# Setup folded into the first layer, and its conditioning groups dealt out anew

## The chip, the cores and the metric

One core of a Trainium2 chip runs the whole program. The metric is the device time of one execution in microseconds; the median of three is what is compared. TensorE (PE) multiplies, VectorE (DVE), ScalarE (ACT) and GpSimd (POOL) do the rest, SyncE (SP) issues most loads.

## What is computed

Two blocks of a network over 512 tokens of width 1024, all in float32. The first block projects x into 28 tiles of 128 features and mixes them in five ways (a short gated convolution, a spatial gating unit, a multi-scale pooling, a 31-tap convolution, an attention over 256 memory tokens), gates the result and projects it out. The second block conditions its norms on a vector c, and this is what the change moves about:

```python
cond = jax.nn.silu(c)
for layer in range(DEPTH_2):
    mod = (cond @ ada_w[layer] + ada_b[layer])[:, None, :]
    shift1, scale1, gate1, shift2, scale2, gate2 = jnp.split(mod, 6, axis=-1)
    hn = rmsnorm(x, norm1_w[layer]) * (1 + scale1) + shift1
```

`cond @ ada_w` for both layers is, for the two layers together, a vector times a 1024 x 12288 matrix that is read once; the kernel computes it in twelve groups of 1024 outputs, off TensorE, beside other stages.

## The kernel before

The program is a row of stages, each a block of five instruction streams (one for each engine) with a boundary behind it: no engine enters a stage before all have left the last. `stage_setup` (L420) loads memory, key/value weights and x from SP, seventeen small tables from ACT, clears tables in device memory from POOL, and takes the Silu of c once all small tables are there. `stage_first` (L511) makes keys and values (4 blocks of weights), then 28 projections of one weight block each (`project`, 16 matmuls, float32 in two passes); between them PE does the small products of the five mixers in an order written out by hand, and ACT (`take`) and DVE follow in orders of their own. `stage_out` (L904) is the output projection in eight blocks, then a layer norm and a first RMS norm. `stage_ffn` (L1356) is the feed-forward with its own seven conditioning groups.

Weights stream through a ring of eight slots, filled by SP in order of use: `load_first` (L183) gives the first eight orders, each behind the use that frees its slot. PSUM's banks 0 and 1 take the projections in turn, banks 2 to 7 the small products.

A conditioning group is eight chunks of weights (128 x 1024, 512 KB), each multiplied by one element of `cond` per partition and added to a sum. On DVE (`weigh`, L484) a chunk is one instruction (L490; the first of a group L488), on POOL two (L580, L581; the first L578). Chunks lie in four buffers; two of them share their place with the memory tile, so that their loads wait for the last key/value block. A finished sum goes over PE: `spread_sums(c)` issues eight narrow products (sixteen matmuls, L506), and `finish_conditioning` (L493) adds the bias on DVE. Before the change, in the first layer DVE makes group 0 before anything else and POOL groups 1 to 4, with two buffers for the sums, so that POOL's group c (from 2 on) waits until group c-2 has been spread.

DVE's order in the first layer: group 0; the input product (L829) and the taps of the long convolution (L800, two instructions a tap) with softmax(0) and softmax(1) between them (L808 to L814); `norm_v.centre` (L320); the pooling (L819 to L859); `norm_v.invert` (L324) and the scaling of v (L862 to L864), which PE's `turn_values` (L643) waits for; then the rest. PE's `turn_probs(j)` (L624) waits for softmax(j).

Of the kernel before, what the change touches and what calls it, by code (L numbers as in the profile page):

```python
# [11 lines left out]
P = 128  # L12
S = 512
ST = S // P
# [93 lines left out]
class Chip:  # L108


    def __init__(self, nc, ctx):
# [42 lines left out]
        self.vlink, self.alink, self.glink, self.plink = (Link(self.sem(n)) for n in  # L154
                                                          ("dve_step", "act_step", "pool_step", "pe_step"))
# [264 lines left out]
def stage_setup(m, a):  # L420
    nc = m.nc
    m.s_small, m.s_x, m.s_mem, m.s_gel, m.s_const = (m.sem(n) for n in ("small_loaded", "x_loaded", "mem_loaded",
                                                                        "table_loaded", "consts_set"))
    m.s_zero = m.sem("table_cleared")
    m.memT = m.W[:, 14:18, :].rearrange("p a (b c) -> p (a b) c", c=MEM)
    with nc.Block() as block:  # L426
        @block.sync
        def _(sp):
            sp.dma_start(m.memT, a["memT"]).then_inc(m.s_mem, 16)
            load_first(m, sp, m.plans["kv"])  # L430
            sp.dma_start(m.X[:], a["xT"]).then_inc(m.s_x, 16)

        @block.scalar
        def _(act):
            for out, src in ((m.par[:], a["par"]), (m.cst[:], a["cst"]), (m.lvl[:], a["lvl"]), (m.sel[0:HEADS], a["sel"]),
                             (m.sel[32:32 + HEADS], a["sel"]),
                             (m.sgw[:], a["sgw"]), (m.plw[0:64, 0, 0:64], a["plw"][0]),
                             (m.plw[64:128, 0, 64:128], a["plw"][1]), (m.plw[0:64, 1, 0:64], a["plw"][2]),
                             (m.plw[64:128, 1, 64:128], a["plw"][3]), (m.pw[:], a["pw"]), (m.gw[:], a["gw"]),
                             (m.rw[:], a["rw"])):  # L440
                act.dma_start(out, src).then_inc(m.s_small, 16)

            for h in range(4):
                act.dma_start(m.sgb[64 * (h % 2):64 * (h % 2) + 64, h // 2, :],
                              a["sgb"][h].partition_broadcast(64)).then_inc(m.s_small, 16)
            m.n_small = 17 * 16
            act.wait_ge(m.s_small, m.n_small)
            nc.scalar.activation(m.cond[:], m.p("c"), ACT.Silu).then_inc(m.alink.sem, 1)
            m.alink.n += 1
            act.wait_ge(m.alink.sem, m.alink.n)  # L450

        @block.vector
        def _(dve):
            step = m.vlink.on(dve)
            for t, v in ((m.ones128, 1 / P), (m.ones256, 1 / DG), (m.ones1024, 1 / D), (m.ones, 1.0)):
                step(nc.vector.memset(t[:], v))

        @block.gpsimd
        def _(pool):
            step = m.glink.on(pool)  # L460
            for lo, j in ((0, 64), (64, 0)):
                step(nc.gpsimd.memset(m.plw[lo:lo + 64, :, j:j + 64], 0.0))

            for r in range(EXPERTS):
                step(nc.gpsimd.memset(m.rank_caps[:, r:r + 1], float(CAPS[r])))
                step(nc.gpsimd.memset(m.rank_first[:, r:r + 1], float(FIRST[r])))
            step(nc.gpsimd.memset(m.zero[:], 0))
            pool.dma_start(m.d_tokens.rearrange("(e r) o -> e (r o)", e=EXPERTS), m.zero[:]).then_inc(m.s_zero, 16)
            blank = m.W[0:ROWS - sum(CAPS), 0:2, :]
            step(nc.gpsimd.memset(blank, 0.0))  # L470
            for rest in [m.d_first[FIRST[-1]:, :]] + [m.d_result[p * ROWS + sum(CAPS):(p + 1) * ROWS, :]
                                                      for p in range(PASSES - 1)]:
                pool.dma_start(rest, blank.rearrange("p a c -> p (a c)")).then_inc(m.s_zero, 16)
            pool.wait_ge(m.s_zero, 16 * (1 + PASSES))


# [4 lines left out]
GROUPS, EARLY_GROUPS = 12 * D // COND, 5  # L481
# [29 lines left out]
def stage_first(m):  # L511
# [20 lines left out]
    mx, nmx, rs, ri = ((lambda h, i=i: stat(h, i)) for i in range(4))  # L532
    chunk_in = m.chunk_in = [m.sem(f"cond_loaded{i}") for i in range(CHUNKS)]
    m.chunk_used, m.acc_ready, m.acc_done = (m.sem("cond_" + n) for n in ("used", "summed", "out"))
    chunk_used, acc_ready, acc_done = m.chunk_used, m.acc_ready, m.acc_done
# [6 lines left out]
    with nc.Block() as block:  # L542
        @block.sync
        def _(sp):
            load_first(m, sp, inn)
            load_rest(m, sp, inn)
            load_first(m, sp, out)

        @block.gpsimd
        def _(pool):  # L550
            step = m.glink.on(pool)
            for h in range(4):
                last = nc.gpsimd.tensor_tensor(m.sgw[:, h, :], m.sgw[:, h, :], m.c("tri"), ALU.mult)
                give(pool, last, masked, h + 1)
            step(nc.gpsimd.memset(m.gates_w[:], 0.0))
            for j in range(2):
                step(nc.gpsimd.tensor_copy(m.gates_w[:, :, 32 * j:32 * j + HEADS], m.gw[:, :, rows(j, HEADS)]))
# [3 lines left out]

            load(0)
            load(1)
            pool.wait_ge(m.blocks_done, kv.done + kv.n)
            load(2)
            load(3)
            for n in range(CHUNKS, KD + CHUNKS):
                pool.wait_ge(chunk_used, n - CHUNKS + 1)
                load(n)
            for c in range(1, EARLY_GROUPS):  # L570
                if c >= 2:
                    pool.wait_ge(acc_done, c - 1)
                for k in range(KD):
# [8 lines left out]
                    if n + CHUNKS < EARLY_GROUPS * KD:  # L582
                        load(n + CHUNKS)
# [3 lines left out]
        def _(pe):  # L587
# [31 lines left out]
            def turn_probs(j):  # L619
                for i in range(2):  # L620
# [78 lines left out]
            project(CA)  # L699
            norm_c.var(m, pe)  # L700
            project(CA + 1)
# [3 lines left out]
            project(GATES[1])  # L705
            pointwise()
            for name in GATES[2:6]:
                project(name)
            spread_sums(3)
            for name in GATES[6:]:  # L710
                project(name)
            spread_sums(4)

        @block.scalar
        def _(act):
            step = m.alink.on(act)
            for b in range(4):
# [36 lines left out]
            for name in (DA, DA + 1, DGT, DGT + 1, Q, Q + 1):  # L754
                take(name)
            exps(0)
            take(V)
            take(V + 1)
            take_probs(0)
            take(U)  # L760
            take_attended(0)
            exps(1)
            take(U + 1)
            take(XC)
            take_probs(1)
# [1721 lines left out]
```

## Time and profile before

| | us |
|---|---|
| median of 3 runs | 2237.7 |
| lowest, highest | 2235.6, 2239.43 |
| the profiled execution, its own time | 2241.91 |
| its span | 2239.6 |
| PE busy | 2143.4 |
| DVE busy | 717.2 |
| ACT busy | 518.1 |
| POOL busy | 438.8 |

The times of the views are microseconds from the start of the span. A line of a timeline gives start, length, engine, line of the kernel, operation, output and inputs, shape, count, and in brackets how long the engine had been idle and what released it. Neighbouring instructions of one form are merged; the length then covers them all. The granted clock of TensorE is a share of 2.4 GHz.

### The profile page before, as it was taken

What the parts mean: (1) busy time and instruction counts of PE and PEld (TensorE: products, weight loads), DVE (VectorE), ACT (ScalarE), POOL (GpSimd) and SP (SyncE); (2) the same over time, 40 slices, a digit from 0 to 9 for tenths busy, and PEclk for the clock granted to TensorE, in tenths of its full rate; (3) what the DMA queues carried; (4) which work ended last, traced back from release to release, by engine and by line L of the source; (5) the groups of instructions that cost most, each with busy time, mean ns of one, the idle gap of its engine ahead of it and who ended that gap; (6) DMA issues with size and microseconds to landing.
All of it is one profiled execution on the core that took longest, in us unless ns stands there. A gap on an engine that the chain in (4) does not pass through costs nothing. (4 is left out here: it accounts for less than half of the span.)

```text
span 2239.6 us, 24940 instructions
## 1 busy us (share of the span) xinstructions
PE 2143.4 (96%) x9870; PEld 1441.3 (64%) x9870; DVE 717.2 (32%) x966; ACT 518.1 (23%) x885; POOL 438.8 (20%) x367
## 2 busy tenths in 40 slices
PE   5898999999999999999999999999999999999997
PEld 3343445556554444446444667675599999999996
DVE  1786212345562232320002466676210000000013
ACT  0231001434332000000002666753112111111101
POOL 2829921100001111100000444453120000000011
PEclk9999998899999999997999999999999999999998
DMA  7524331111103555522211211110196577778882
GB/s 282 192 73 132 115 111 46 38 48 57 57 29 113 163 194 191 193 87 105 75 61 56 67 48 57 53 42 19 66 319 196 191 248 236 232 267 296 316 337 97
DMA packets 81230, 308.18 MB, mean 138 GB/s; under 512 B 9832, under 2 KB 10352, under 8 KB 80864
## 3 DMA queue, kind: packets, MB, share of 16 engines
q1 hardware_dynamic: 60768, 238.05, 31.5%
q0 software_dynamic: 16800, 59.87, 8.0%
q10 hardware_dynamic: 3552, 8.74, 1.1%
q8 instruction: 76, 1.25, 0.2%
q14 instruction: 34, 0.28, 0.0%
HBM read 297.30 MB, written 9.33 MB: 137 GB/s over the span
## 5 line engine op out<-in xcount | busy, mean ns | idle before, releaser
L244 PE MATMUL banks<-sb_x_norm,sb_ring 128*128 128x512 f32 x1344 | 588.8, 597 | 3.9 <-ACT sb_x_norm L401 3.9
L2092 PE MATMUL banks<-sb_act,sb_ring 128*128 128x192 f32 (+3 forms) x3696 | 502.9, 299 | 3.0 <-issue 2.9
L2092 PEld LDWEIGHTS banks<-sb_act,sb_ring 128*128 128x128 f32 x3696 | 500.0, 191 | 4.5 <-issue 4.2
L244 PEld LDWEIGHTS banks<-sb_x_norm,sb_ring 128*128 128x128 f32 x1344 | 254.1, 191 | 312.2 <-issue 309.2
L244 PE MATMUL banks<-sb_x_res,sb_ring 128*128 128x512 f32 x448 | 197.0, 598 | 0.0
L2370 DVE TENSOR_TENSOR sb_act<-sb_work,banks 128x128 f32<-128x128 f32 (+3 forms) x88 | 27.7, 315 | 518.0 <-PE banks L2092 496.4
L244 PE MATMUL banks<-sb_act,sb_ring 128*128 128x512 f32 x352 | 153.4, 599 | 3.1 <-PEq L1367 3.1
L244 PEld LDWEIGHTS banks<-sb_x_res,sb_ring 128*128 128x128 f32 x448 | 85.5, 193 | 104.8 <-issue 104.8
L356 POOL TENSOR_TENSOR sb_work<-sb_work 128x512 f32<-128x512 f32 x18 | 22.8, 1265 | 555.7 <-ACT sb_work L348 555.7
L244 PEld LDWEIGHTS banks<-sb_act,sb_ring 128*128 128x128 f32 x352 | 67.6, 192 | 88.1 <-issue 88.1
L255 PEld LDWEIGHTS banks<-sb_ring,sb_x_norm 128*128 128x128 f32 x1024 | 116.0, 192 | 2.5 <-issue 2.4
L255 PE MATMUL banks<-sb_ring,sb_x_norm 128*128 128x128 f32 x1024 | 117.0, 275 | 0.0
L1016 PE MATMUL banks<-sb_act,sb_ring 128*128 128x512 f32 x256 | 112.4, 594 | 0.4 <-DVE sb_act L1752 0.4
L244 PE MATMUL banks<-sb_work,sb_ring 128*128 128x512 f32 (+1 forms) x192 | 81.1, 588 | 27.2 <-PEq L426 25.3
L1964 POOL DMA_INDIRECT sb_work<-first_expert_rows,sb_table x8 | 7.5, 938 | 463.8 <-DMA first_expert_rows<-sb_x_norm 461.7
L2199 ACT ACTIVATE sb_work<-banks 128x128 f32<-128x128 f32 (+3 forms) x88 | 26.3, 298 | 308.5 <-PE banks L2092 306.0
L1709 POOL TENSOR_TENSOR sb_act<-sb_act 128x512 f32<-128x512 f32 x56 | 80.6, 1438 | 65.6 <-PE banks L1554 28.4
L1695 POOL TENSOR_TENSOR sb_act<-sb_act 128x512 f32<-128x512 f32 x56 | 60.6, 1083 | 145.6 <-DVE sb_act L1759 93.8
L1016 PEld LDWEIGHTS banks<-sb_act,sb_ring 128*128 128x128 f32 x256 | 47.8, 190 | 61.2 <-issue 59.4
L1413 DVE TENSOR_TENSOR sb_act<-sb_work,banks 128x512 f32<-128x512 f32 x22 | 15.1, 686 | 213.9 <-PE banks L244 213.9
L244 PEld LDWEIGHTS banks<-sb_work,sb_ring 128*128 128x128 f32 x192 | 39.0, 204 | 68.2 <-issue 66.8
L1554 PEld LDWEIGHTS banks<-sb_act 128*128 128x128 f32 x512 | 62.7, 192 | 24.8 <-issue 17.1
(368 smaller groups left out, 2158.8 us busy)
## 6 DMA issues: line engine op xcount, KB each, us to landing
sb_ring<-in_w_moe_up SPq DMA_DIRECT2D x176, 512.0 KB
sb_ring<-in_w_moe_down SPq DMA_DIRECT2D x64, 704.0 KB
sb_work<-in_cond_w POOLq DMA_DIRECT2D x48, 512.0 KB, 4.7
sb_ring<-in_w_ffn_up SPq DMA_DIRECT2D x44, 512.0 KB
sb_ring<-in_w_h_in SPq DMA_DIRECT2D x32, 512.0 KB
sb_ring<-in_w_in SPq DMA_DIRECT2D x28, 512.0 KB
sb_act<-in_cond_w POOLq DMA_DIRECT2D x28, 512.0 KB, 4.9
sb_ring<-in_w_m_in SPq DMA_DIRECT2D x24, 512.0 KB
```

What stands on the lines that cost most here:

```text
L244: last = m.nc.tensor.matmul(bank[:, 0:act.shape[2]], w[:, rows(k, P)], act[:, k, :], start=(k == 0), stop=(k == kt - 1))
L255: last = m.nc.tensor.matmul(bank[:, rows(t, P)], act[:, k, rows(t, P)], w[:, rows(k, P)], start=(k == 0), stop=(k == kt - 1))
L356: m.nc.gpsimd.tensor_tensor(self.acc, self.acc, self.sq[:, k % 2, :], ALU.add).then_inc(m.rms_sum, 1)
L1016: last = m.nc.tensor.matmul(m.ps[:, b % BANKS, :], m.ring[:, s, rows(k, P)], act_in[:, k, :], start=(k == 0), stop=(k == kt - 1))
L1413: nc.vector.tensor_tensor(out, W[:, s % 2:s % 2 + 1, :], ps[:, (2 * s + 1) % BANKS:(2 * s + 1) % BANKS + 1, :], ALU.mult).then_inc(m.evac, 2)
L1554: last = nc.tensor.matmul(ps[:, 2 + n % 2, rows(t, P)], lhs[:, rows(t, P)], rhs[:, rows(t, P)], start=True, stop=True)
L1695: give(pool, nc.gpsimd.tensor_tensor(H[:, n % 2, :].rearrange("p (n c) -> p n c", c=2 ** j), b, b[:, :, half - 1:half].broadcast_to([P, S ...
L1709: give(pool, nc.gpsimd.tensor_tensor(H[:, 4 + n % 2, :], k_of(h), H[:, n % 2, :], ALU.mult), k_ready, n)
L1964: nc.gpsimd.indirect_dma_start(got[2 * t + j], None, table, bass.IndirectOffsetOnAxis(ap=m.table[:, c:c + 1], axis=0)).then_inc(gathered[t ...
L2092: last = nc.tensor.matmul(ps[:, b % BANKS, 0:cap], w, act, start=(k == 0), stop=(k == kt - 1))
L2199: nc.scalar.activation(silu_t[j % 2][:, 0:cap], ps[:, 2 * j % BANKS, 0:cap], ACT.Silu).then_inc(silu, 1)
L2370: nc.vector.tensor_tensor(hid[:, j, 0:cap], silu_t[j % 2][:, 0:cap], ps[:, (2 * j + 1) % BANKS, 0:cap], ALU.mult).then_inc(m.evac, 2)
```

## The change

`stage_setup` is gone. Its loads stand at the head of `stage_first`: SP's before the projection weights; ACT's in two parts, `par` and `cst` at once, the other tables behind the memory tile, and `lvl`, `sel` and `rw` not before `stage_out`. POOL's clearing of tables goes to `stage_out`. Engines wait for the tables by semaphores of their own (`s_par`, `s_small`, `s_x`, `s_cond`). In the first layer POOL makes groups 0 to 2 and DVE none; DVE makes groups 3 and 4 in `stage_out`, three chunks behind each block, with loads issued by ACT; PE spreads them behind block 6. The feed-forward keeps seven. The orders of PE, ACT and DVE in the first layer shift: each small product comes about one projection later relative to the blocks, softmax(0) comes after `taps(1, 5)`, softmax(1) after `taps(5, 16)`, `norm_v.centre` after `taps(16, 26)`, and v is finished before most of the pooling. In the experts' stage four semaphores are merged into others. The core of it:

```diff
 stage_first, sync
+            sp.dma_start(m.memT, a["memT"]).then_inc(m.s_mem, 16)
+            load_first(m, sp, kv)
+            sp.dma_start(m.X[:], a["xT"]).then_inc(m.s_x, 16)
             load_first(m, sp, inn)
 stage_first, gpsimd
+            pool.wait_ge(m.s_x, 16)
+            load(0)
+            load(1)
+            pool.wait_ge(m.s_small, N_SMALL)
...
-            for n in range(CHUNKS, KD + CHUNKS):
-                pool.wait_ge(chunk_used, n - CHUNKS + 1)
-                load(n)
-            for c in range(1, EARLY_GROUPS):
+            pool.wait_ge(m.s_cond, 1)
+            for c in range(FIRST_GROUPS):
 stage_first, tensor
             project(V + 1)
+            project(U)
             turn_probs(0)
-            project(U)
+            project(U + 1)
             attend(0)
             scores(1)
-            project(U + 1)
             project(XC)
+            project(XC + 1)
             turn_probs(1)
-            project(XC + 1)
+            project(XA)
             attend(1)
             norm_v.mean(m, pe)
             spread_sums(0)
             spread_sums(1)
-            project(XA)
+            project(XA + 1)
             norm_v.var(m, pe)
-            project(XA + 1)
             project(BA)
+            project(BA + 1)
             turn_values()
-            project(BA + 1)
+            project(CA)
             gating()
...
-            spread_sums(3)
...
-            spread_sums(4)
 stage_first, scalar
+            act.dma_start(m.par[:], a["par"]).then_inc(m.s_par, 16)
+            act.dma_start(m.cst[:], a["cst"]).then_inc(m.s_small, 16)
+            act.wait_ge(m.s_par, 16)
+            nc.scalar.activation(m.cond[:], m.p("c"), ACT.Silu).then_inc(m.s_cond, 1)
+            act.wait_ge(m.s_mem, 16)
...
 stage_first, vector
-            for k in range(KD):
-                dve.wait_ge(chunk_in[k % CHUNKS], 16 * (k // CHUNKS + 1))
-                weigh(m, step, chunk[k % CHUNKS], sums[0], k)
-                dve.sem_inc(chunk_used, 1)
-            dve.sem_inc(acc_ready, 1)
-            taps(1, 9)
+            taps(1, 5)
             softmax(0)
-            taps(9, 16)
+            taps(5, 16)
             softmax(1)
-            taps(16, TAPS_D - 1)
+            taps(16, 26)
+            norm_v.centre(m, dve)
+            taps(26, TAPS_D - 1)
 stage_out, tensor
+            def spread_sums(b):
+                if b == KD - 2:
+                    for c in range(FIRST_GROUPS, EARLY_GROUPS):
+                        pe.wait_ge(m.acc_ready, c + 1)
+                        spread_group(m, sums[c - FIRST_GROUPS], 7, c).then_inc(m.acc_done, 1)
 stage_out, vector
             for b in range(plan.n):
...
+                for n in range(per * b, min(per * (b + 1), loads)):
+                    conditioning(n)
+                if b == KD - 2:
+                    dve.wait_ge(m.acc_done, EARLY_GROUPS)
+                    finish_conditioning(m, step, FIRST_GROUPS, EARLY_GROUPS,
+                                        ps[:, 7, 8 * FIRST_GROUPS:8 * EARLY_GROUPS], ((0, 1, "norm2"),))
 stage_out, scalar
+            for n in range(loads):
+                if n >= CHUNKS:
+                    act.wait_ge(m.chunk_used, n - CHUNKS + 1)
+                act.dma_start(chunk[n % CHUNKS], m.cond_w[begun + n]).then_inc(chunk_in[n % CHUNKS], 16)
             nc.scalar.preload_act_table(ACT.Sqrt)
```

## Rows read from the trace of the kernel before

**Rows 1.** The page: busy time and share of the engines.
```profile
PE 2143.4 (96%) x9870; PEld 1441.3 (64%) x9870; DVE 717.2 (32%) x966; ACT 518.1 (23%) x885; POOL 438.8 (20%) x367
```
**Rows 2.** Waits of TensorE, 0 to 400 us: total, times, longest.
```profile
PE banks L643 <- DVE sb_act L864: 10.4, 1, 10.4
PE banks L624 <- DVE sb_act L814: 8.8, 2, 7.4
```
**Rows 3.** Timeline of TensorE, 20 to 300 us.
```profile
25.30 9.39 PE L244 MATMUL banks<-sb_work,sb_ring 128*128 128x256 f32 x32 [25.30 <-PEq L426]
41.67 18.62 PE L244 MATMUL banks<-sb_x_res,sb_ring 128*128 128x512 f32 x43
...
83.73 2.00 PE L614 MATMUL banks<-sb_act 64*128 64x256 f32 x16 [0.69 <-ACT sb_act L730]
...
107.10 1.97 PE L624 MATMUL banks<-sb_cst,sb_act 128*128 128x128 f32 x8 [7.44 <-DVE sb_act L814]
...
120.65 1.94 PE L635 MATMUL banks<-sb_act 128*64 128x512 f32 x8
...
187.11 1.97 PE L643 MATMUL banks<-sb_cst,sb_act 128*128 128x128 f32 x8 [10.37 <-DVE sb_act L864]
...
293.33 1.95 PE L506 MATMUL banks<-sb_ones,sb_x_norm 128*128 128x1 f32 x16
297.19 71.75 PE L244 MATMUL banks<-sb_work,sb_ring 128*128 128x512 f32 x160 [1.91 <-PEq L542]
```
**Rows 4.** Timeline of ScalarE: the Silu in setup.
```profile
24.46 0.21 ACT L448 ACTIVATE sb_cond<-sb_par 128x8 f32<-128x8 f32 x1 [11.69 <-DMA sb_sgb<-in_sgb]
```
**Rows 5.** DMA, 0 to 25 us: traffic; size and us from issue to landing.
```profile
DMA packets 2768, 7.97 MB, mean 319 GB/s; under 512 B 808, under 2 KB 1328, under 8 KB 2512
...
sb_x_res<-in_xT SPq DMA_DIRECT2D x1, 2048.0 KB, 18.8
sb_work<-in_memT SPq DMA_DIRECT2D x1, 1024.0 KB, 5.5
```
**Rows 6.** Timeline of VectorE, 69 to 156 us.
```profile
69.97 2.15 DVE L829 TENSOR_TENSOR sb_act<-sb_act 128x1024 f32<-128x1024 f32 x1 [9.01 <-ACT sb_act L730]
...
74.01 25.47 DVE L800 SCALAR_TENSOR_TENSOR sb_work<-sb_act,sb_par,sb_work 128x511 f32<-128x511 f32 x16
...
110.42 10.81 DVE L800 SCALAR_TENSOR_TENSOR sb_work<-sb_act,sb_par,sb_work 128x503 f32<-128x503 f32 x14
124.63 1.23 DVE L808 TENSOR_REDUCE sb_small<-banks 128x4 f32<-128x1024 f32 x1 [3.40 <-PE banks L614]
...
133.75 22.10 DVE L800 SCALAR_TENSOR_TENSOR sb_work<-sb_act,sb_par,sb_work 128x496 f32<-128x496 f32 x28
```
**Rows 7.** Timeline of GpSimd: the first instruction of groups 1, 2 and 3.
```profile
61.99 2.85 POOL L578 TENSOR_SCALAR sb_x_norm<-sb_x_norm,sb_cond 128x1024 f32<-128x1024 f32 x1
...
152.63 2.92 POOL L578 TENSOR_SCALAR sb_x_norm<-sb_x_norm,sb_cond 128x1024 f32<-128x1024 f32 x1 [42.44 <-PE banks L506]
...
200.14 2.86 POOL L578 TENSOR_SCALAR sb_x_norm<-sb_x_norm,sb_cond 128x1024 f32<-128x1024 f32 x1
```
**Rows 8.** Timeline of VectorE: inside the pooling, inverse of v, last gate.
```profile
165.13 0.69 DVE L852 COPY sb_work<-sb_act 64x512 f32<-64x512 f32 x1
...
178.13 3.35 DVE L324 RECIPROCAL sb_act<-sb_act 128x512 f32<-128x512 f32 x1
...
293.99 0.69 DVE L898 TENSOR_TENSOR sb_work<-sb_work,sb_act 128x512 f32<-128x512 f32 x1 [5.91 <-ACT sb_act L730]
```
**Rows 9.** Window behind a stall: length, busy PE, PEld, DVE, ACT, POOL, clock, DMA.
```profile
107.10:112.20 5.10, 3.72 (x16) 3.32 (x17) 4.07 (x5) 4.04 (x8) 2.80 (x2) 0.50 0.20 48
```
**Rows 10.** Timeline of TensorE: two spreads.
```profile
150.68 3.63 PE L506 MATMUL banks<-sb_ones,sb_x_norm 128*128 128x1 f32 x32
```
**Rows 11.** Timeline of VectorE: a weighing; the page: loads of chunks.
```profile
50.62 1.28 DVE L490 SCALAR_TENSOR_TENSOR sb_x_norm<-sb_work,sb_cond,sb_x_norm 128x1024 f32<-128x1024 f32 x1 [1.33 <-DMA sb_work<-in_cond_w]
...
sb_work<-in_cond_w POOLq DMA_DIRECT2D x48, 512.0 KB, 4.7
```

More of the change, by code:

```diff
@@ L417 @@
 YA, YB, YC, YD, YE = 0, 2, 4, 6, 8
[L420 to L474, printed above, removed]
@@ L551, in _, with load @@
             step = m.glink.on(pool)
+            for lo, j in ((0, 64), (64, 0)):
+                step(nc.gpsimd.memset(m.plw[lo:lo + 64, :, j:j + 64], 0.0))
+            for r in range(EXPERTS):
+                step(nc.gpsimd.memset(m.rank_caps[:, r:r + 1], float(CAPS[r])))
+                step(nc.gpsimd.memset(m.rank_first[:, r:r + 1], float(FIRST[r])))
+            step(nc.gpsimd.memset(m.gates_w[:], 0.0))
+            def load(n):
+                pool.dma_start(chunk[n % CHUNKS], m.cond_w[n]).then_inc(chunk_in[n % CHUNKS], 16)
+            pool.wait_ge(m.s_x, 16)
+            load(0)
+            load(1)
+            pool.wait_ge(m.s_small, N_SMALL)
             for h in range(4):
@@ L619, in turn_probs @@
             def turn_probs(j):
+                if j == 0:
+                    pe.wait_ge(m.s_small, N_SMALL)
                 for i in range(2):
@@ L705, in _ @@
             project(GATES[1])
+            project(GATES[2])
             pointwise()
-            for name in GATES[2:6]:
+            for name in GATES[3:6]:
                 project(name)
-            spread_sums(3)
             for name in GATES[6:]:
                 project(name)
-            spread_sums(4)
         @block.scalar
@@ L787, in _ @@
             give(act, last, conv_act, 1)
-            for name in GATES[1:]:
+            for name in GATES[2:]:
                 take(name)
@@ L909, in stage_out @@
     total, sq = m.W[:, 12, :], m.W[:, 13:15, :]
+    wide = lambda t: t.rearrange("p a c -> p (a c)")
+    chunk = [wide(m.A[:, 2 * i:2 * i + 2, :]) for i in range(CHUNKS)]
+    sums = [wide(m.A[:, 2 * i:2 * i + 2, :]) for i in range(CHUNKS, CHUNKS + EARLY_GROUPS - FIRST_GROUPS)]
+    chunk_in = [m.sem(f"ln_cond_loaded{i}") for i in range(CHUNKS)]
+    begun, loads, per = FIRST_GROUPS * KD, (EARLY_GROUPS - FIRST_GROUPS) * KD, 3
     std, inv = m.small[:, 48:48 + ST], m.small[:, 52:52 + ST]
@@ L920, in _ @@
         def _(pool):
+            step = m.glink.on(pool)
+            step(nc.gpsimd.memset(m.zero[:], 0))
+            pool.dma_start(m.d_tokens.rearrange("(e r) o -> e (r o)", e=EXPERTS), m.zero[:]).then_inc(m.s_zero, 16)
+            blank = m.W[0:ROWS - sum(CAPS), 15:17, :]
+            step(nc.gpsimd.memset(blank, 0.0))
+            for rest in [m.d_first[FIRST[-1]:, :]] + [m.d_result[p * ROWS + sum(CAPS):(p + 1) * ROWS, :]
+                                                      for p in range(PASSES - 1)]:
+                pool.dma_start(rest, blank.rearrange("p a c -> p (a c)")).then_inc(m.s_zero, 16)
             for k in range(1, KD - 1):
@@ L958, in _, with conditioning @@
         def _(dve):
+            step = m.vlink.on(dve)
+            def conditioning(n):
+                c, k = divmod(n, KD)
+                dve.wait_ge(chunk_in[n % CHUNKS], 16 * (n // CHUNKS + 1))
+                weigh(m, step, chunk[n % CHUNKS], sums[c], k)
+                dve.sem_inc(m.chunk_used, 1)
+                if k == KD - 1:
+                    dve.sem_inc(m.acc_ready, 1)
             for b in range(plan.n):
@@ L1885, in stage_moe @@
         "last_slots", "last_slots_turned", "last_slots_out", "early_turned", "last_mixed", "added", "early_mixed"))
-    gathered = [m.sem(f"e_early{t}") for t in range(ST)]
     got_sem = [m.sem(f"e_gathered{i}") for i in range(BUFS)]
@@ L2329, in mix @@
             def mix(t, turn):
-                dve.wait_ge(gathered[t], 32 * turn)
+                for i in (2 * t, 2 * t + 1):
+                    dve.wait_ge(got_sem[i], 16 * ((1 if turn == 1 else PASSES) * got_used[i] - (i == 0) + turn))
                 a1, a2 = got[2 * t], got[2 * t + 1]
```

93 lines of the change are left out of this document (54 added, 39 removed).

## The prediction

> **What bounds the kernel now.** The page first: TensorE (PE) is busy 96% of a 2239.6 us span [rows 1]. Time can come only from PE's gaps or its work, and the change leaves PE's work as it is: the same blocks, the same twelve groups of conditioning. So the question is which gaps lie in the three stages touched, the first 400 us. PE's waits there name two behind VectorE (DVE): 10.4 us at L643 (`turn_values`) and 8.8 us at L624 (`turn_probs(0)`) [rows 2]; its timeline adds a third, 25.30 us before the first matmul. It projects from 41.67, and begins the output stage at 297.19 [rows 3]. The first gap is the block boundary behind setup: the Silu of ScalarE (ACT) waits until 24.46 for the last small table [rows 4], and PE starts 0.84 us later. What PE itself needs, the memory tile and weight block 0, was there long before: the memory tile landed 5.5 us after its order, at about 6.4 [rows 5]. The other two gaps are a late DVE: from 69.97 it hardly rests, and its taps take 25.47/16 = 1.59 us each while GpSimd (POOL) computes, but 22.10/28 = 0.79 us while it is idle [rows 6, 7].
>
> I count from T0, the first projection (41.67 in the old trace). A block of 16 matmuls is 6.87 us: six take 83.73 - 0.69 - 41.67 = 41.4 with the last one's tail [rows 3].
>
> **The head.** PE now needs the memory tile (6.4) and block 0 of the key weights, 0.52 MB behind it in the same queue. The first 25 us moved 0.319 MB/us on average [rows 5]: 1.6 us alone, 3.3 us if ACT's tables take half, so PE starts between 8.0 and 9.7; I take 8.5. Its four key/value blocks take 41.67 - 25.30 = 16.4 us [rows 3], so T0 = 24.9, 16.8 earlier. What this hides must be there in time. The input X: ahead of it or beside it go 1.05 MB (memory), 2.1 (weights), 2.1 (X itself) and 1.5 (ACT's tables), 6.75 MB, at 0.319 MB/us 21 us, against 24.9. Without that cover T0 moves one for one. ACT's orders of the tables: all seventeen ended by 24.46 - 11.69 = 12.8 us, a table load included [rows 4]; now eleven of them start behind the memory tile, which bounds their end by 6.4 + 12.8 = 19 and, by their share, puts it at 14; ACT's first copy of keys is due at 14.5, and PE's fourth block would be the first to feel it. Setup's memsets on DVE and POOL lie beside loads: nothing.
>
> The Trainium skill's "DMA: Bandwidth & Descriptors", under Queues, rings and completion order, says that each DMA engine serves the queues it has work for in turn, a packet at a time. By it ACT's tables could take up to half of block 0's turns, and PE would start at 9.7, not 8.5: the sum would be 1.2 us smaller.
>
> **Three groups on POOL, none on DVE in the first stage.** DVE loses eight weighings, but it sat idle for 9.01 us before L829, waiting for a projection [rows 6], so that buys nothing. POOL began its first group 20.3 us behind the old T0 (61.99); now it begins when the key/value blocks are done and two chunks are ordered, 1 us behind T0. A group takes 200.14 - 152.63 = 47.5 us [rows 7]. It computes from T0+1 to T0+96 without a rest, where before it did from T0+20 to T0+68 and again from T0+111. So DVE's taps meet it longer.
>
> **DVE's chain in the new order, from T0.** The projection it starts from is ready at 69.97 - 41.67 = 28.3. Products and bias, 74.01 - 69.97 = 4.0 -> 32.3. `taps(1,5)`, 8 instructions at 1.59 = 12.7 -> 45.0. The scores are there at 83.73 + 2.00 - 41.67 = 44.1, so softmax(0) runs at once: 110.42 - 99.48 = 10.9 -> 55.9. PE wants its probabilities after one more block than before, at 64.9: that gap is closed. `taps(5,16)`, 22 at 1.59 = 35.0 -> 90.9, all beside POOL. Softmax(1): 133.75 - 124.63 = 9.1 beside an idle POOL, 10.9 beside a busy one [rows 6]; half of it is beside POOL, and the higher is nearer as ACT loads a table in it: 10.9 -> 101.8. `taps(16,26)`, 20 at 0.79 = 15.8 -> 117.6: POOL is idle, its third group waiting for `spread_sums(0)` at 117.5 (below). Centring, one pass over 128x1024 out of PSUM like L808 (1.23) -> 118.8. `taps(26,30)`, 8 at 1.59 -> 131.5. The last two taps and two doublings: 165.13 - 155.85 = 9.3 held these and a centring, so 8.1 -> 139.6. Inverse and scaling of v, 187.11 - 178.13 = 9.0 -> 148.6 [rows 3, 8]. The rest of the pooling, 178.13 - 165.13 = 13.0, now stands behind v.
>
> **PE against it.** PE comes to 73.5 through `turn_probs(0)` (1.75) and one more block, attend and scores(1), 3.8 -> 77.3, two blocks -> 91.0. There `turn_probs(1)` needs probabilities whose softmax only begins at 90.9: the old gap again, at the other half. The old one took 120.65 - (107.10 - 7.44) = 21.0 us for 8.6 us of work (transposes 1.75, a block 6.87) [rows 3]; part of its price is the clock, 0.50 of 2.4 GHz in the 5.1 us behind that idleness [rows 9]. Taken over: loss 12.4, PE at 112.0. Attend 1.9, a mean about 1.8, two spreads 3.6 [rows 3, 10] -> 119.3 (the first spread ends at 117.5), three blocks and a variance 22.3 -> 141.6. `turn_values` waits for DVE until 148.6: 7.0 us. So the stage's end hangs on DVE: from `turn_values` to the last block the old PE took 293.33 - 187.11 = 106.2 [rows 3], now one block (6.87) and one spread (1.8) less: 97.6 -> 246.2. POOL's third group ends at T0 + 117.5 + 47.5 = 165, before PE asks for it at 179.
>
> **Into the output stage.** Behind the last block ACT and DVE still take 294.68 - 293.33 = 1.35 us [rows 8], then three small steps instead of five and the boundary, 1.91 less 0.4 [rows 3]: 2.9. Start: 24.9 + 246.2 + 2.9 = 274.0 against 297.19, 23.2 earlier. There two spreads stand between blocks 6 and 7: 3.63 us of PE [rows 10]. DVE gets three weighings of 1.28 a block besides its 0.7, 4.5 us in 71.75/8 = 9.0 of PE's block: hidden; without that cover each of six blocks would wait. Chunks land in 4.7 us [rows 11] and are ordered a block ahead (four buffers, three used a block) by ACT, whose own work there is the norm behind block 7; the last of its sixteen orders waits for the twelfth chunk, in block 3. POOL clears tables before its first addition, under blocks 0 and 1. In the experts' stage only the semaphore waited for changes; the feed-forward keeps seven groups. Nothing for either.
>
> **Sum.** -23.2 + 3.6 = -19.6 us. The profiled execution took 2241.91 us for a span of 2239.6, the median of the runs is 2237.7, and a difference of spans holds for either: 2237.7 - 19.6 = 2218.1.
>
> **Bounds.** PE's start 8.0 to 9.7, or 12 if its first instructions come slowly; softmax(1) 9.1 to 10.9; 38 contended taps, four of which fit one turn of POOL's two instructions, so that a phase is worth a tap at each change of neighbour, in all some 4 us either way; the clock's share of the loss 0 to 4.8 (12.4 - 7.44 and rounding). Together 2209 to 2227.
>
> **Rivals.**
> (a) *VectorE is held up less.* If contention cost nothing, both PE gaps close and PE's own work decides: 12.4 + 7.0 = 19.4 more, 2198.7. For it: the free tap of 0.79. Against it: the same two forms of instruction met from 74 to 99.5 and a tap took 1.59.
> (b) *The loads don't come in order.* If the first weight block lands only with the whole stream, at 21 us, PE starts 4.3 us earlier, not 16.8: 2230.6. Against it: the memory tile landed in 5.5 us where X, behind it, took 18.8 [rows 5].
> (c) *DVE's chain is 10 to 20 us longer*, since more of it stands beside POOL than before and contended operations scatter: 2228 to 2238. No row asks for it.
> (d) *Slower.* DVE loses each GpSimd instruction entire. It would then get two operations into a turn of POOL's two instructions (47.5/8 = 5.9 us, 6.4 beside taps) where the trace shows four: 3.2 us a tap, 61 us more for 38 taps, 2279. It decides from about 20 us of added delay, 13 such taps. Against it: 1.59 a tap is in the rows with the same neighbour [rows 6, 7].
> The Trainium skill's "SBUF — State Buffer", Who interferes with whom, states the rule of (d): the two engines share a pair of ports under a lock held for a whole instruction, and the loser fully blocks. The trace agrees that they meet, but not that a whole instruction is lost each time.
> (e) *The head's change does nothing*: no wait is left in front of PE but the tile and the block, so no chance of its own.
>
> **Chances.** Forecast 0.72, (a) 0.10, (b) 0.06, (c) 0.09, (d) 0.03. To hold eight in ten the range takes the forecast's bounds and the near parts of (a) and (c): 2207 to 2229. A measurement of this kernel tells 0.2% (4.5 us) from no change. Faster: the forecast, (a), (b) and half of (c), 0.92; same 0.05; slower 0.03.
>
> **What would show it.** First matmul at 8.5, T0 at 25; no gap at `turn_probs(0)`, one of about 8 us at `turn_probs(1)` with a granted clock near 0.5 behind it, 7 us at `turn_values`; taps at 1.59 until POOL's second group ends; the output stage from 274, two spreads between its blocks 6 and 7 without a wait; all later stages shifted as they are. It is wrong if the first projection waits for X, PE for POOL's third group, or a block of the output stage for DVE.

## The result and the profile after

The changed kernel takes 2219.8 us (median of 4, 2217.5 to 2224.0) where the kernel before, beside it, takes 2236.65 (2235.3 to 2239.4): the medians stand 16.9 us apart. This document goes by the ratio of the executions, 0.9919, with a 95% interval of 0.9901 to 0.9937, which is 18.1 us of 2237 (14.1 to 22.1); it is not the quotient of the medians, here or below. The forecast was 2218.1 with 2207 to 2229. The profiled execution took 2218.68 us for a span of 2217.0.

The page's busy time of each engine, to be held against rows 1: TensorE (PE) does what it did and 2.8 us more, VectorE (DVE) 17.6 us more, GpSimd (POOL) 42.7 us less.

```profile
PE 2146.2 (97%) x9870; PEld 1441.9 (65%) x9870; DVE 734.8 (33%) x975; ACT 517.2 (23%) x884; POOL 396.1 (18%) x336
```

The waits of PE from 0 to 400 us: total, times, longest. Rows 2 had 10.4 and 8.8 us behind DVE and, in front of all, the 25.30 us of rows 3. Now it is 8.9 for the first weights, 8.1 at `turn_probs` (L580) and 2.6 at `turn_values` (L599).

```profile
PE banks L243 <- DMA sb_ring<-in_w_kv: 8.9, 1, 8.9
PE banks L580 <- DVE sb_act L783: 8.1, 2, 7.7
PE banks L243 <- PEq L488: 3.2, 1, 3.2
PE banks L599 <- DVE sb_act L824: 2.6, 1, 2.6
```

PE's timeline shows where these stand (start, length, and in brackets the idle time and its releaser):

```profile
8.93 10.14 PE L243 MATMUL banks<-sb_work,sb_ring 128*128 128x256 f32 x32 [8.93 <-DMA sb_ring<-in_w_kv]
...
26.04 41.37 PE L243 MATMUL banks<-sb_x_res,sb_ring 128*128 128x512 f32 x96
...
124.94 1.97 PE L580 MATMUL banks<-sb_cst,sb_act 128*128 128x128 f32 x8 [7.71 <-DVE sb_act L783]
...
144.21 8.81 PE L243 MATMUL banks<-sb_x_res,sb_ring 128*128 128x512 f32 x16
...
171.11 1.17 PE L599 MATMUL banks<-sb_cst,sb_act 128*128 128x128 f32 x8 [2.65 <-DVE sb_act L824]
...
271.95 63.23 PE L243 MATMUL banks<-sb_work,sb_ring 128*128 128x512 f32 x140 [3.18 <-PEq L488]
335.02 3.63 PE L449 MATMUL banks<-sb_ones,sb_act 128*128 128x1 f32 x32
338.51 10.53 PE L243 MATMUL banks<-sb_work,sb_ring 128*128 128x512 f32 x20
```

The first projection (T0) starts at 26.04 instead of 41.67, the output stage at 271.95 instead of 297.19 [rows 3]: 25.2 us earlier. Of that 7.0 go again before `stage_m`, the mixer behind the output stage: its first full block starts at 398.13, against 416.37 before (18.2 earlier). The feed-forward's first block is as much earlier (703.56 against 721.74), and so are the late blocks of the experts' stage (up to 2123.36 against 2141.41). The spans stand 22.6 us apart; the 4.5 us more arise behind that point, in a tail of 98.2 us before and 93.6 now, with 2.0 us less waiting of PE (9.3 and 7.3 us from 2000 us on). In the ten further traces below, all with the changed experts' stage, this tail takes 92.2 to 96.9 us, so most of the 4.5 is scatter; whether the four merged semaphores add to it, no run separates.

DVE's timeline:

```profile
58.66 12.74 DVE L769 SCALAR_TENSOR_TENSOR sb_work<-sb_act,sb_par,sb_work 128x511 f32<-128x511 f32 x8
71.44 1.22 DVE L777 TENSOR_REDUCE sb_small<-banks 128x4 f32<-128x1024 f32 x1
72.69 2.34 DVE L778 TENSOR_SCALAR sb_small<-sb_small 128x4 f32<-128x4 f32 x1
...
82.74 35.32 DVE L769 SCALAR_TENSOR_TENSOR sb_work<-sb_act,sb_par,sb_work 128x507 f32<-128x507 f32 x22
...
127.31 15.28 DVE L769 SCALAR_TENSOR_TENSOR sb_work<-sb_act,sb_par,sb_work 128x496 f32<-128x496 f32 x20
142.63 1.22 DVE L319 TENSOR_TENSOR sb_act<-sb_act,banks 128x1024 f32<-128x1024 f32 x1
143.77 10.60 DVE L769 SCALAR_TENSOR_TENSOR sb_work<-sb_act,sb_par,sb_work 128x486 f32<-128x486 f32 x8
```

Here and below a tap is one instruction; the kernel's `taps(a, b)` issues two for each step, so `taps(5, 16)` is 22. A tap costs 12.74/8 = 1.59 and 35.32/22 = 1.61 us beside POOL, 15.28/20 = 0.76 beside an idle one. POOL's group 2 starts at T0 + 116.6, released by a spread:

```profile
142.66 2.84 POOL L532 TENSOR_SCALAR sb_x_norm<-sb_x_norm,sb_cond 128x1024 f32<-128x1024 f32 x1 [18.03 <-PE banks L449]
```

In the output stage three weighings a block take 4.92 us, dearer than 3 x 1.28, and DVE still idles over 3 us before the next block:

```profile
309.47 0.69 DVE L960 SCALAR_TENSOR_TENSOR sb_x_res<-sb_x_res,banks 128x512 f32<-128x512 f32 x1 [3.50 <-PE banks L243]
310.07 4.92 DVE L433 SCALAR_TENSOR_TENSOR sb_act<-sb_act,sb_cond 128x1024 f32<-128x1024 f32 x3
```

### The profile page after: what moved, and what is told of

It reads as the page before. It is cut to its first block and busy times, and to the rows that moved or that the text cites. A ratio compares the mean times of both kernels' runs of the same rounds, so it can differ in the third digit from the quotient of the medians.

```text
span 2217.0 us, 24937 instructions
## 1 busy us (share of the span) xinstructions
PE 2146.2 (97%) x9870; PEld 1441.9 (65%) x9870; DVE 734.8 (33%) x975; ACT 517.2 (23%) x884; POOL 396.1 (18%) x336
## 5 line engine op out<-in xcount | busy, mean ns | idle before, releaser
L1567 PEld LDWEIGHTS banks<-sb_act 128*128 128x128 f32 x512 | 62.7, 192 | 25.1 <-issue 17.4
```

Source lines behind the costliest of these rows:

```text
L1567: last = nc.tensor.matmul(ps[:, 2 + n % 2, rows(t, P)], lhs[:, rows(t, P)], rhs[:, rows(t, P)], start=True, stop=True)
```

## The experiments

The theory: three things make up the gain and the loss. The head gives 16 us; DVE is held up by POOL and so keeps PE waiting twice; the spreads moved to the output stage cost there what they cost. Rivals: head and order don't add up, since one hides the other; the two stalls are a matter of DVE's order, not of POOL. Ratios are to the kernel before, run beside each, with 95% intervals. Edits are shown against the changed kernel, and only their core.

**e1_head_alone**: the changed kernel's head, with the groups and the orders of before.

```diff
-GROUPS, FIRST_GROUPS, EARLY_GROUPS = 12 * D // COND, 3, 5
+GROUPS, FIRST_GROUPS, EARLY_GROUPS = 12 * D // COND, 5, 5
...
-            taps(1, 5)
+            taps(1, 9)
```

> The kernel before with only the loads merged into the first stage (POOL's clearing in the output stage too); DVE makes group 0, POOL groups 1 to 4, all orders of the first stage as before. My theory: the head and the rest add up, and relative to the first projection nothing changes. First matmul at 8.9, first projection at 26.0 as in the changed kernel (15.6 earlier than 41.67), gaps of about 8.8 and 10.4 us at turn_probs(0) and turn_values remain, ratio to before 2222/2237.7 = 0.993 (0.9925 to 0.9935). Rival: the head is worth more or less with the old dealing, because POOL and DVE now work beside a DMA queue that is still full at the head; then the gaps differ from 8.8 and 10.4 by more than 2 us.

Measured: 2229.19 us, 0.9947 (0.9927 to 0.9967), 11.9 us (7.4 to 16.3), less than expected. T0 comes at 25.80, 15.9 us earlier, but the output stage only 13.6 and `stage_m`'s first block 14.8:

```profile
95.83 3.65 PE L583 MATMUL banks<-sb_cst,sb_act 128*128 128x128 f32 x16 [12.05 <-DVE sb_act L786]
...
172.89 1.97 PE L602 MATMUL banks<-sb_cst,sb_act 128*128 128x128 f32 x8 [8.68 <-DVE sb_act L841]
...
283.58 70.60 PE L243 MATMUL banks<-sb_work,sb_ring 128*128 128x512 f32 x160 [1.81 <-PEq L488]
```

The wait at `turn_probs(0)` is 12.05 us where rows 3 have 7.44 with a second one of 1.4 behind it: 3.2 us more, which is what the rival named (over 2 us). POOL works beside that softmax in both kernels, but DVE meets other instructions of it. Counted from T0, PE gets its probabilities 4.6 us later: 1.2 us because the first product takes 3.32 us for 2.15, 1.4 us in a wait for ScalarE (1.78 for 0.43), and 2.0 us because the first scaling of the probabilities takes 3.21 us for 1.22. From T0 to the output stage it is 257.8 us against 255.5. So in this trace the head's gain isn't passed on whole while the old order stands.

**e2_head_undone**: the rest of the change, with its loads in a block of their own ahead of the first layer (the tables `lvl`, `sel` and `rw` and the clearing stay in the output stage).

```diff
+    with nc.Block() as block:
+        @block.sync
+        def _(sp):
+            load_first(m, sp, inn)
...
+            act.wait_ge(m.s_cond, 1)
+            act.wait_ge(m.s_x, 16)
```

> The changed kernel with the head's loads in a block of their own that ends when they have landed; new groups and orders kept. My theory: first matmul at about 20 to 25, and every later time relative to the first projection as in the changed kernel; the rest of the change is worth 18.1 - 15.6 = 2.5 us, ratio to before 0.998 to 0.9995. Rival: regrouping and orders are what pays, then the ratio is under 0.996.

Measured: 2230.11 us, 0.997 (0.9949 to 0.9991), 6.7 us (2.0 to 11.4), between the forecast and its rival. Its ten executions reach from 2227.7 to 2241.9 us, four of them above 2235. PE starts at 21.41: the block for setup alone is 3.9 us shorter than the old one.

```profile
21.41 8.95 PE L243 MATMUL banks<-sb_work,sb_ring 128*128 128x256 f32 x32 [21.41 <-PEq L488]
...
136.18 1.97 PE L610 MATMUL banks<-sb_cst,sb_act 128*128 128x128 f32 x8 [7.65 <-DVE sb_act L801]
```

11.9 and 6.7 us make 18.6, the whole change 18.1: within the intervals, which are wide, the parts add up, and nothing here speaks for parts that hide one another. Some 3.9 us of e2's gain is that shorter block, not order or groups, which by the ratios leaves these about 3. The trace says more: from T0 to `stage_m`'s first block e2 takes 364.6 us where the kernel before takes 374.7, so 10.1 less, and the changed kernel's two traces 372.1 and 365.7 (the second is e8's, below). What order and groups bring by themselves is therefore open between some 3 and 10 us.

**e3_light_gpsimd**: in chunks 1 to 7 of its groups 0 and 1 POOL computes 128 of 1024 columns (the rest of the conditioning of these chunks is left out), with the same loads and waits.

```diff
                     else:
+                        if c < 2:
+                            src, total = src[:, 0:P], total[:, 0:P]
```

> The changed kernel, but in groups 0 and 1 POOL multiplies and adds only the first 128 of 1024 columns of chunks 1 to 7 (that part of the conditioning is left out); loads, waits and the third group stay. My theory: POOL's work beside DVE is what makes DVE late. Taps near 0.79 us until the third group, the softmax of heads 2 and 3 done before PE asks, both PE gaps (7.7 + 0.4 and 2.65 us) closed and the slower clock behind them gone: the first stage ends 13 to 16 us earlier, ratio to the changed kernel's 0.9919 lower by 0.006 to 0.007, so about 0.985 to before. Rival: DVE is late by its order, not by POOL; then at least 5 us of the gap at turn_probs(1) stays.

Measured: 2207.35 us, 0.9857 (0.9829 to 0.9886), as forecast. POOL is through with the two groups at 66.2 us, the same 22 taps take half, and PE finds its probabilities and v ready:

```profile
69.94 0.17 DVE L780 TENSOR_SCALAR sb_small<-sb_small 128x4 f32<-128x4 f32 x1
...
77.81 17.07 DVE L771 SCALAR_TENSOR_TENSOR sb_work<-sb_act,sb_par,sb_work 128x507 f32<-128x507 f32 x22
101.89 1.22 DVE L779 TENSOR_REDUCE sb_small<-banks 128x4 f32<-128x1024 f32 x1 [7.02 <-PE banks L570]
```
```profile
115.54 1.91 PE L582 MATMUL banks<-sb_cst,sb_act 128*128 128x128 f32 x16
...
155.74 1.09 PE L601 MATMUL banks<-sb_cst,sb_act 128*128 128x128 f32 x8
...
254.89 63.37 PE L243 MATMUL banks<-sb_work,sb_ring 128*128 128x512 f32 x140 [3.19 <-PEq L488]
```

From T0 (24.52) to the output stage it is 230.4 us against 245.9. With the order unchanged, both stalls go when POOL's work goes: they are POOL's doing, and this is what is left to win in the stage, 15.5 us.

**e4_second_softmax_early**: softmax(1) ten taps earlier, to close the wait at `turn_probs(1)`.

```diff
-            taps(5, 16)
+            taps(5, 11)
             softmax(1)
-            taps(16, 26)
+            taps(11, 26)
```

> The changed kernel with taps(5,11) before softmax(1) and taps(11,26) behind it, nothing else. My theory: the end of the first stage hangs on the whole of DVE's chain to v, not on each gap by itself. The gap at turn_probs(1) closes (PE 11 us earlier there), POOL's third group starts 11 us earlier and so lies beside more taps, v is ready 0 to 8 us later than 171.1, and PE waits for it at turn_values for 14 to 22 us instead of 2.65: ratio to before 0.992 to 0.996, no better than the changed kernel. Rival: each gap has its own price, and closing this one gives 8 to 11 us: ratio 0.987 to 0.988.

Measured: 2229.88 us, 0.9951 (0.9935 to 0.9968). The wait is gone, and two others, of 19.6 us together, stand behind it (PE's waits, 0 to 400 us):

```profile
PE banks L292 <- ACT sb_act L304: 11.1, 1, 11.1
PE banks L243 <- DMA sb_ring<-in_w_kv: 9.1, 1, 9.1
PE banks L599 <- DVE sb_act L824: 8.6, 1, 8.6
```

The earlier attend lets the spread through earlier, so POOL's third group starts at 131 and holds up DVE's thirty taps (36.35 us), and the centring behind them is late for `norm_v.var` (L292). I had put the whole delay at `turn_values`; the place was wrong, the size (19.6 against 14 to 22) and the ratio were not. The rival, that each gap has a price of its own (0.987 to 0.988), falls.

**e5_two_groups** and **e6_two_groups_reordered**: only groups 0 and 1 in the first layer, group 2 on DVE in the output stage; e6 also places softmax(1), the centring and the finishing of v where PE wants them.

```diff
-GROUPS, FIRST_GROUPS, EARLY_GROUPS = 12 * D // COND, 3, 5
+GROUPS, FIRST_GROUPS, EARLY_GROUPS = 12 * D // COND, 2, 5
...
-            spread_sums(2)
...
-    begun, loads, per = FIRST_GROUPS * KD, (EARLY_GROUPS - FIRST_GROUPS) * KD, 3
+    begun, loads, per = FIRST_GROUPS * KD, (EARLY_GROUPS - FIRST_GROUPS) * KD, 4
```
```diff
# e6 beside that; v's inverse, product and scaling move up
-            taps(5, 16)
+            taps(5, 11)
             softmax(1)
-            taps(16, 26)
+            taps(11, 18)
             norm_v.centre(m, dve)
-            taps(26, TAPS_D - 1)
+            taps(18, 25)
+            norm_v.invert(m, dve)
...
+            taps(25, TAPS_D - 1)
```

> The changed kernel with two groups on POOL in the first stage and three on DVE in the output stage (four weighings a block instead of three). My theory: the gap at turn_values was POOL's third group beside the chain to v, that at turn_probs(1) the first two. So the first stays (7 to 8 us at turn_probs(1)), the gap of 2.65 at turn_values closes, v is ready 8 to 12 us earlier than 171.1, the output stage's DVE still keeps up (0.7 + 4 x 1.28 = 5.8 of 8.6 us a block): 2.5 to 4.5 us better than the changed kernel run beside it, 0.998 to 0.999 of it. Rival: DVE can't hide a third group in the output stage, a block waits there, and it is slower than the changed kernel by 3 us or more.

> As the run with two groups, and DVE's order changed: taps(5,11), softmax(1), taps(11,18), centring of v, taps(18,25), inverse and scaling of v, the other taps, pooling. My theory (the chain as a whole is what counts, and it is now short enough): both gaps and the wait for the centred v that showed when softmax(1) alone was moved are closed, PE has no wait above 1 us between its first projection and the output stage, which starts 11 to 15 us earlier than in the changed kernel: ratio to before 0.985 to 0.988. Rival: as with softmax(1) moved alone, the time comes back as another wait behind DVE, and the gain over the changed kernel is under 5 us.

Measured: e5 2218.83 us, 0.9916 (0.9902 to 0.9931); e6 2207.99, 0.9865 (0.9851 to 0.988). The changed kernel beside them (e8, below) has 0.9928 (0.9915 to 0.9941), so e6's gain over it is shown by the times, some 14 us, and e5's isn't. In e5 the wait at `turn_values` is gone and that at `turn_probs(1)` stays (6.4 us); from T0 to the output stage it takes 238.4 us where e8 takes 245.7, and that stage gives 3.4 us back with its third group. In e6 both are gone: PE waits at no place longer than 0.7 us between T0 and the output stage, which starts 17.2 us earlier than e8's (271.29; I had expected 11 to 15). At `stage_m`'s first block 7.4 of them are left (383.87 against 391.28). Three spreads stand in a row in e6's output stage, and the block behind them takes 11.47 us, where the seven before it took 61.7/7 = 8.8 each.

```profile
254.12 61.73 PE L243 MATMUL banks<-sb_work,sb_ring 128*128 128x512 f32 x140 [3.17 <-PEq L488]
315.68 7.75 PE L449 MATMUL banks<-sb_ones,sb_act 128*128 128x1 f32 x48
323.29 11.47 PE L243 MATMUL banks<-sb_work,sb_ring 128*128 128x512 f32 x20
```

**e7_spreads_split** and **e8_changed_again**: the changed kernel with no two spreads in a row, and the changed kernel itself beside it.

```diff
             spread_sums(0)
-            spread_sums(1)
             project(XA + 1)
             norm_v.var(m, pe)
             project(BA)
+            spread_sums(1)
...
-                if b == KD - 2:
-                    for c in range(FIRST_GROUPS, EARLY_GROUPS):
+                if b in (KD - 4, KD - 2):
+                    c = FIRST_GROUPS + (b == KD - 2)
```

> The changed kernel with its two pairs of spreads taken apart: spread_sums(1) two blocks after spread_sums(0), group 3's spread behind block 4 of the output stage and group 4's behind block 6. Theory: 3.6 us of narrow matmuls in a row are often followed by a block at a lower granted clock (8.7 instead of 6.9 us, 10.4 instead of 8.6), a single spread of 1.8 us never was. The blocks behind spreads then take 6.9 and 8.6, and the kernel is up to 3.6 us faster than the changed one beside it. Rival: the slow blocks fall where they fall and have nothing to do with the narrow matmuls; then some block near by is as slow, and nothing is gained.

> The changed kernel itself, as the measure for the three beside it on the same chip: ratio to before 0.990 to 0.994 again.

Measured: e7 2218.05, 0.9912 (0.9899 to 0.9925); e8 2221.38, 0.9928 (0.9915 to 0.9941). The medians stand 3.3 us apart and the intervals overlap, so the times decide nothing. In the trace no block behind a single spread is slow (7.11, 7.11, 17.41 for two, 8.83), but `turn_values` waits 4.35 us instead of 2.81: DVE ends there when it did, and a faster PE only comes sooner. Nor did the output stage get shorter in this trace: its first five blocks, ahead of any spread, took 45.87/5 = 9.2 us each where e8's first seven took 60.16/7 = 8.6, and the eight blocks with their spreads 75.2 us against 74.0. So e7 shows no gain, neither in its time nor in its trace.

**e9_both** and **e10_reordered_again**: e6 with each spread by itself (in the first layer by e7's edit), and e6 again beside it, where no stall behind DVE can swallow the gain.

```diff
-                if b == KD - 2:
-                    for c in range(FIRST_GROUPS, EARLY_GROUPS):
+                if b in (KD - 6, KD - 4, KD - 2):
+                    c = FIRST_GROUPS + (b - 2) // 2
```

> As e6_two_groups_reordered (2207.99), but no two spreads stand in a row: in the first layer spread_sums(1) behind project(BA), in the output stage one spread each behind blocks 2, 4 and 6. Theory (a row of narrow products makes the clock of the block behind it drop): that block goes from about 11.5 to about 7 us in the output stage and from 8.7 to 7.1 in the first layer, 4 to 6 us in all less the 0 to 1.5 that TensorE may now wait: 0.9950 to 0.9985 of e6 in the same call, about 0.984 of the kernel before. Rival (the clock is taken from TensorE somewhere anyway, whatever stands between the blocks): within 0.1% of e6, with other blocks slower instead. VectorE's slack at turn_values is 1 us or less in e6, so a new wait there over 2 us would mean a later centring, not the clock.

> The kernel of e6_two_groups_reordered once more, beside e9_both: 0.985 to 0.988 of the kernel before. The block behind the three spreads of the output stage takes 10 to 12 us again if the spreads cause it, 8.6 or less if it was chance.

Measured: e9 2203.87 (2197.1 to 2207.8), 0.9856 (0.984 to 0.9873); e10 2209.08 (2204.2 to 2212.8), 0.9867 (0.985 to 0.9883). The medians stand 5.2 us apart and the ratios 0.0011 (2.5 us), and the intervals again overlap. Against e10 that is 0.9976 by the medians, inside the 0.9950 to 0.9985 expected, and 0.9989 by the ratios, outside. PE's timeline of e9, then of e10:

```profile
129.79 7.11 PE L243 MATMUL banks<-sb_x_res,sb_ring 128*128 128x512 f32 x16
...
278.70 1.84 PE L449 MATMUL banks<-sb_ones,sb_act 128*128 128x1 f32 x16
280.40 17.41 PE L243 MATMUL banks<-sb_work,sb_ring 128*128 128x512 f32 x40
...
318.31 8.83 PE L243 MATMUL banks<-sb_work,sb_ring 128*128 128x512 f32 x20
```
```profile
131.73 8.81 PE L243 MATMUL banks<-sb_x_res,sb_ring 128*128 128x512 f32 x16
...
313.21 7.58 PE L449 MATMUL banks<-sb_ones,sb_act 128*128 128x1 f32 x48
320.66 11.65 PE L243 MATMUL banks<-sb_work,sb_ring 128*128 128x512 f32 x20
```

The windows of these blocks (length; busy PE, PEld, DVE, ACT, POOL; granted clock; DMA share; GB/s), e9's two and then e10's two:

```profile
129.79:136.74 6.95, 6.95 (x18) 3.13 (x18) 6.63 (x10) 0.94 (x1) 0.00 (x0) 1.00 0.00 0
...
318.31:326.98 8.67, 8.67 (x23) 3.89 (x23) 0.58 (x3) 0.00 (x0) 0.59 (x1) 1.00 0.14 52
```
```profile
131.73:140.38 8.65, 8.65 (x18) 3.73 (x18) 8.21 (x12) 0.00 (x0) 0.00 (x0) 0.80 0.00 0
...
320.66:332.15 11.49, 11.49 (x22) 4.97 (x23) 0.52 (x3) 0.00 (x0) 0.00 (x0) 0.75 0.00 0
```

The block behind a spread is 7.11 instead of 8.81 in the first layer and, behind the last spread of the output stage, 8.83 instead of 11.65 at a granted clock of 1.00 instead of 0.80 and 0.75 (my "about 7" for that one was a slip: such a block has 20 matmuls and takes 8.6 undisturbed). `turn_values` doesn't wait. T0 to the output stage is 1.65 us shorter and the eight blocks with their spreads 75.74 against 79.10, so 5.0 us in the trace, what the theory asked for; but e9's first three blocks were slower than e10's (27.46/3 = 9.2 against 60.16/7 = 8.6), at a clock of 0.94 and 1.00, with nothing in the code that sets them apart. As e7's first blocks were slow too, one could think that the time is taken elsewhere when the spreads are apart. Against it: the changed kernel and e3, with their spreads in a row, had both the slow first seven blocks (9.0 us each) and the slow block behind. That separated spreads leave the next block alone is shown; that the kernel is 5 us faster by it isn't, by these intervals. Either version, e6 or e9, beats both kernels of this case.

## Why the prediction was right, point by point

*The head.* PE starts at 8.93 us, in the range 8.0 to 9.7, 0.4 later than I took. The four key/value blocks took 17.1 instead of 16.4, so T0 moved 15.6, not 16.8. The first two of them took 8.58 to 10.14 us over the executions of this head, at a granted clock of 1.00 and with no wait in the records; what makes them differ stays open. The covers held: POOL's wait for X ends at 19.33 and ACT's table orders at 12.8, both before they are wanted. The loads came in order; (b) falls. PE's start lies between the two values that I gave for the first block, alone or sharing its turns with ACT's tables (8.5, 9.7), so the rule of the queues' turns is neither shown nor refuted.

*DVE's chain.* Taps beside POOL 1.59 and 1.61 us for 1.59; softmax(0) 11.3 for 10.9; softmax(1) 9.2 for 10.9, mostly because its two small scalings (L778) took 0.27 and 0.43 us for softmax(0)'s 2.34 and 0.77, though POOL was at work beside these too, until 123.7: a busy POOL has no one price; free taps 15.3 for 15.8. The last eight contended taps took 10.60 where I had 12.7; POOL begins its group there with a single instruction and a load order before the steady turn of two, and the same eight took 7.50 in e3 and 11.53 in e4. v is ready at T0 + 145.1, 3.5 us before the forecast. That lies within the 4 us that the bounds gave to scatter, so (a) and (c) fall. That contention is the cause of both stalls, e3 shows.

*PE against it.* No wait at `turn_probs(0)`, 7.71 + 0.42 at `turn_probs(1)`; the loss from it, with a slower clock, is 11.2 us (137.03 - 117.23 - 8.6) where I took over 12.4. The window (length; busy PE, PEld, DVE, ACT, POOL; clock; DMA) repeats the 0.50 of rows 9:

```profile
124.94:129.10 4.16, 3.73 (x17) 3.33 (x17) 3.11 (x5) 2.88 (x7) 0.00 (x0) 0.50 0.39 128
```

PE comes to `turn_values` at T0 + 142.4 (141.6 forecast) and waits 2.65 instead of 7.0. From there to the end of the last block 97.66 us, as forecast (97.6), then 3.2 to the output stage (2.9).

*The output stage.* The spreads cost their 3.63 us, as forecast, and DVE's weighings are hidden, though dearer than their 1.28. What I missed is the block behind the spreads: 10.36 us to its end where the seven before took 63.07/7 = 9.0, at a clock of 0.84:

```profile
338.51:348.87 10.36, 10.36 (x23) 4.45 (x22) 0.51 (x3) 0.00 (x0) 0.00 (x0) 0.84 0.00 0
```

With 1.6 us more in the layer norm's narrow products behind it, the way from the stage's start to `stage_m`'s first block is 126.2 us against 119.2 before: 7.0 where I had 3.6. So the terms were off in both directions: the head gave 1.2 us less, the way from T0 to the output stage 3.2 more, the output stage cost 7.0 for 3.6, and 19.6 became 18.2. In e8, another execution of the same kernel, that last way took 120.0 us: the 3.4 of excess are within what the clock does from one execution to the next. There `stage_m`'s first block comes at 391.28, 25.1 us earlier than before, and the stretch from it to the feed-forward, which the change leaves alone, takes 313.6 us where the other trace has 305.4. So the mechanism and the first layer's size are right by the traces, whose way from T0 to the output stage agrees to 0.2 us (245.9 and 245.7); that the total comes within 2 us of the forecast is partly luck: the errors of its terms cancel in part, and the interval of the measured difference is 4 us either way.

*The rival (d)* falls. A tap, shorter than a POOL instruction (0.77 against 2.85 and 2.5 us), was on average held up 0.83 us. Seven taps of one stretch, by DVE's line (duration in ns, min/median/max):

```profile
L769 DVE SCALAR_TENSOR_TENSOR sb_work<-sb_act,sb_par,sb_work x7: 740/744/2709, 94.7 to 102.6; 128x503 f32<-128x503 f32 x2, 128x502 f32<-128x502 f32 x2, 128x501 f32<-128x501 f32 x2, 128x504 f32<-128x504 f32 x1
```

Four of them run free at 744 ns at most and three are held, up to 2709. By their starts (94.7, 95.5, 96.3, 99.0, 101.1, 101.9, 102.6) two free ones follow one another, then come a held one of 2.7 us and one of 2.0: four taps to POOL's turn of 6.37 us, half of them free. The 22 taps together have a median of 1388 ns, between the two kinds. So in this stretch a tap is held up either not at all or by 2.0 or 1.3 us. The Trainium skill's "SBUF — State Buffer", Who interferes with whom, says that a VectorE instruction with two SBUF inputs contends with a GpSimd instruction that reads SBUF, that a reduction never does, and that whoever comes second is fully blocked while the other has the ports. The trace agrees on who contends, as far as it goes: the taps are held, and the reduction, which reads PSUM here, takes 1.22 us beside POOL and, in e3, beside an idle one. The small scaling behind it takes 2.34 against 0.17 us, from 72.69 to 75.03 beside POOL's addition from 72.67 to 75.02: there one instruction is blocked for the whole of the other. The held taps lose less than a whole POOL instruction and half of the taps nothing, where (d) needed the whole for each.

## What to carry to other kernels

Before counting on a gain at the head, follow it to the first engine that has its own schedule: of 15.9 us of earlier start, 13.6 reached the next stage here while VectorE's order stayed. A wait behind a held-up engine took two cures together: moving some of the other engine's work away (e5 alone left 6.4 us of waiting) and placing the steps anew (e4 alone sent the delay to the next customer, 19.6 us of it); e6, which does both, has no such wait left. The full new order with three groups left on GpSimd wasn't run. List all customers of the chain with their due times and place each step by its due time. Narrow products put singly between wide blocks leave the next block alone, though the kernel's time doesn't show the gain here. Compare stages, not spans, when the effect sought is a few microseconds, and know how far each stage scatters by itself.

## What the runs showed of the hardware

**Narrow products in a row slow the block behind them.** A spread is 16 matmuls with one column. Two or three of them in a row were followed by a slower block in 8 of 10 traces in the first layer (8.70 to 8.81 us instead of 7.11; not in before and e2), and in 8 of 8 in the output stage (10.24 to 11.65). Single spreads, 19 of them in nine traces with a block behind, never were. In the changed kernel the granted clock of the two such blocks is 0.80 and 0.84. In before and e2 the block of the first layer had 1.00, and why these two escaped isn't settled.

**The same kernel's clock differs between executions.** The first seven blocks of the output stage took 63.07 us at a clock of 0.95 in one execution of the changed kernel and 60.16 at 1.00 in another (e8), and `stage_m`'s first block came at 398.13 and 391.28. The windows of the two, after and e8:

```profile
271.95:335.02 63.07, 63.07 (x141) 27.76 (x142) 26.18 (x22) 1.28 (x1) 14.38 (x11) 0.95 0.69 244
```
```profile
271.29:331.45 60.16, 60.16 (x141) 26.68 (x142) 26.28 (x22) 1.28 (x1) 14.39 (x11) 1.00 0.72 255
```

The clock fell in another place in e8: from `stage_m`'s first block to the feed-forward it is 0.97 and 313.6 us there, 1.00 and 305.4 in the other. A difference below about 8 us in one of these stages in a pair of traces proves nothing of the code by itself. The first layer is steadier: from T0 to the output stage the two traces differ by 0.2 us, and those of e6 and e10, one kernel too, by 0.1. The Trainium skill's "TensorE: Matmul & The Clock Gate", Part 1, says that the number of one kernel's slow matmuls at its start differs from run to run; here the clock differs in the middle of a program too.

**GpSimd pays little beside the taps, and more beside the weighings.** Beside `taps(5, 16)` its addition took 2.47 to 2.59 us instead of 2.35, while a tap went from 0.77 to 1.61 on average. In the output stage its addition of 512 columns took 2.17 us beside VectorE's weighings and 1.27 without them, while a weighing went from 1.28 to 4.92/3 = 1.64. So who pays depends on the pair of instructions.
